# Two low weight halves moved in among the last residuals of a SwiGLU layer, and an earlier square root table load

## What is computed

```
def swiglu(h, w_in, w_out):
    g, u = jnp.split(h @ w_in, 2, axis=-1)
    return (jax.nn.silu(g) * u) @ w_out
...
x = x + 0.5 * swiglu(rms_norm(x, g), w_in, w_out)      # hidden width 2816
```

## Time and profile before

| what | value |
|---|---|
| median of 3 runs | 2894.66 us (2893.04 to 2894.82) |
| the profiled execution, whole | 2899.12 us |
| its span, first to last instruction | 2897.4 us |
| TensorE matmuls busy | 2780.8 us, 96% of the span |
| VectorE busy | 2065.6 us, 71% |
| ScalarE busy | 1025.2 us, 35% |
| TensorE's mean granted clock | 0.977 of full speed |
| HBM read | 418.94 MB, 145 GB/s over the span |

### The profile page before, as it was taken

The page is one execution under the profiler, slowest core; times in us unless marked ns, Lnnn a source line. Parts: engine busy times, 40 slices in busy tenths (PEclk is TensorE's granted clock), DMA queues, the critical chain, the costliest instruction groups (busy, mean ns, idle before and its releaser), DMA issues.

```text
span 2897.4 us, 49248 instructions
## 1 busy us (share of the span) xinstructions
PE 2780.8 (96%) x19380; PEld 2454.6 (85%) x19380; DVE 2065.6 (71%) x3075; ACT 1025.2 (35%) x1158; POOL 81.4 (3%) x152
## 2 busy tenths in 40 slices
PE   6999999999999999999999899998999999998999
PEld 4888877888878888788799899987799989986999
DVE  6877778867777777776667766656767766665677
ACT  5222224222232222233344444452144434443433
POOL 1000000000000000000000000000000000000000
PEclk9999999999999999999999999999999999998999
DMA  8444441443334444322245344421044544543354
GB/s 327 160 145 168 168 170 59 166 152 130 130 116 160 146 180 171 111 95 74 84 175 187 131 174 174 180 88 60 3 166 175 201 124 174 191 157 66 116 187 175
DMA packets 68705, 421.43 MB, mean 145 GB/s; under 512 B 7672, under 2 KB 8824, under 8 KB 26592
## 3 DMA queue, kind: packets, MB, share of 16 engines
q1 hardware_dynamic: 48032, 341.26, 31.8%
q0 software_dynamic: 20576, 78.78, 8.4%
HBM read 418.94 MB, written 1.07 MB: 145 GB/s over the span
## 4 chain that ended last, share of the span: by engine, by line
PE 86%; DVE 7%; issue 2%; ACT 2%; DMA 1%; DVEq 0%; SPq 0%; ACTq 0%
PE ps_o L2158 11%; PE ps_o L2159 10%; PE ps_o L2160 10%; PE ps_g L2158 7%; PE ps_u L2158 7%; PE ps_u L2159 7%; PE ps_u L2160 7%; PE ps_g L2159 7%; PE ps_g L2160 7%; PE ps_g L2173 2%; DVE wlo L1203 2%; ACT whi L708 1%; DMA wraw<-in_W 1%; PE ps_o L2378 1%; PE ps_o L2364 1%
## 5 line engine op out<-in xcount | busy, mean ns | idle before, releaser
L708 ACT ACTIVATE whi<-wraw 128x2048 fp32r<-128x2048 f32 x323 | 616.2, 1911 | 785.9 <-PE ps_u L2160 367.5
L1203 DVE TENSOR_TENSOR wlo<-wraw,whi 128x2048 fp32r<-128x2048 f32 x323 | 731.5, 2287 | 159.8 <-ACT whi L708 159.5
L2158 PE MATMUL ps_o<-ah,wlo 128*128 128x256 f32 (+1 forms) x1408 | 466.6, 331 | 12.2 <-issue 7.6
L2158 PE MATMUL ps_g<-hh,wlo 128*128 128x256 f32 (+1 forms) x1464 | 464.3, 317 | 12.5 <-ACT tsq L823 7.4
L2158 PE MATMUL ps_u<-hh,wlo 128*128 128x256 f32 (+1 forms) x1464 | 462.1, 316 | 0.3 <-DVE wlo L1203 0.2
L2160 PE MATMUL ps_g<-hh,whi 128*128 128x256 f32 (+1 forms) x1464 | 461.9, 315 | 0.0
L2159 PE MATMUL ps_g<-hl,whi 128*128 128x256 f32 (+1 forms) x1464 | 461.9, 315 | 0.0
L2159 PE MATMUL ps_u<-hl,whi 128*128 128x256 f32 (+1 forms) x1464 | 461.7, 315 | 0.0
L2160 PE MATMUL ps_u<-hh,whi 128*128 128x256 f32 (+1 forms) x1464 | 461.7, 315 | 0.0
L2159 PE MATMUL ps_o<-al,whi 128*128 128x256 f32 (+1 forms) x1408 | 455.6, 324 | 0.0
L2160 PE MATMUL ps_o<-ah,whi 128*128 128x256 f32 (+1 forms) x1408 | 455.4, 323 | 0.0
(11 more groups left out here) (456 smaller groups left out, 3726.6 us busy)
## 6 DMA issues: line engine op xcount, KB each, us to landing
wraw<-in_W SPq DMA_DIRECT2D x324, 1024.0 KB, 4.8
scr<-in_ADA POOLq DMA_DIRECT2D x126, 512.0 KB, 3.7
scr<-bias_rows POOLq DMA_DIRECT2D x8, 384.0 KB, 8.5
x<-in_XT POOLq DMA_DIRECT2D x1, 2048.0 KB, 10.4
x<-in_MEMT POOLq DMA_DIRECT2D x2, 1024.0 KB, 6.3
cst<-in_CST POOLq DMA_DIRECT2D x1, 1511.5 KB, 7.2
cst<-in_CB POOLq DMA_DIRECT2D x1, 1024.0 KB, 5.1
scr<-in_PM POOLq DMA_DIRECT2D x1, 1024.0 KB, 5.1
```

The source lines that it names most:

```text
L708: nc.scalar.activation(whi[:, n % SLOTS, :], wraw[:, n % SLOTS, :], ACT.Copy).then_inc(w_hi, 1)
L1203: tt_(wlo[:, n % SLOTS, :], wraw[:, n % SLOTS, :], whi[:, n % SLOTS, :].bitcast(f32), sub).then_inc(w_lo, 1)
L2158: mm(out, a[1], b[0], start=first, stop=False)
```

## The change

In layers 3 to 7 alone. On ScalarE a one-column square root stands behind the last SiLU of the layer. On VectorE the low half of the next stage's first chunk stands behind residual 3 of `n_down` and not behind residual 7, and the low half of the second stands behind residual 2 of `n_last` and not ahead of its residual 0.

```
                     silu(i * step + DONE[n0 + 2], i + (g0 + 1), i + (lg + 2))
                     if f in LATE:
                         split_hi(n0 + 5, i, step, per)
+                    nc.scalar.activation(cols[:, 61:62], C("eps", 1), ACT.Sqrt)
                     hidden(i + (g0 + 1), last_hi)
                     split_hi(n0 + 6, i, step, per)
                     split_hi(n0 + 7, i, step, per)
...
                     down(n_down, done, range(1))
                     hidden(i + (g0 + 1), last_hi, last_lo)
-                    down(n_down, done, range(1, KT))
+                    down(n_down, done, range(1, 4))
                     split_lo(n_up + SLOTS, i, per)
+                    down(n_down, done, range(4, KT))
+                    down(n_last, DONE[n_last - 1], range(3))
                     split_lo(n_down + SLOTS, i, per)
-                down(n_last, DONE[n_last - 1])
+                    down(n_last, DONE[n_last - 1], range(3, KT))
+                else:
+                    down(n_last, DONE[n_last - 1])
                 st["late"].append(n_last + SLOTS)
```

## The result

| | before | changed | ratio, 95% interval |
|---|---|---|---|
| first comparison, median | 2894.74 us (4 runs) | 2874.31 us (4 runs) | 0.9925 (0.9908 to 0.9942) |
| second comparison, median | 2895.9 us (11 runs) | 2875.35 us (6 runs) | 0.9929 (0.9914 to 0.9944) |
| span of the profiled execution | 2897.4 us | 2873.9 us | |

The change wins 20.4 us in the medians; 22.6 were forecast. To see where, I measure each layer's end alone: from the start of the last product on VectorE (line 1337 before, 1338 after) to the start of the last residual. In layers 3 to 7 that was 19.65, 18.96, 19.25, 18.86 and 15.34 before, and is 15.35, 13.61, 15.27, 13.60 and 12.38 now.

The account below looks back on a forecast made before the run. TensorE bounds 86% of the span, so time is won where it waits or runs at half clock. Layers 3 to 7 give 4.4 + 5.5 + 4.05 + 5.4 + 3.2 = 22.55 off the median 2894.66: 2872.1 us, range 2868 to 2881.

Parts of the forecast that it names:

- What set the wait: Layer ends: VectorE's low halves set TensorE's wait in layers 4 and 6 (2.90 in 4), ScalarE in 3 and 5 (3.54).
- Low B's place: Second chunk's low half behind residual 2 of n_last: runs 1843.04 to 1845.24 in layer 4, no wait at sum 3.
- The new wait at tile 0: First output tile of n_last, layer 4: starts at 1840.38 instead of 1839.89, a wait of 0.49, bounds 0 to 0.6.
- the hand-over from VectorE to TensorE: n_last's first tile in layer 4: TensorE starts it 0.06 behind the end of VectorE's residual 4.
- it would not fall behind 1.6 us: Layers 3 and 5: 1.6 us of idle time stays, TensorE keeps full clock; gains 4.4 and 4.05.
- rival 2: Timed runs lose clock less often than the profiled one: gain 18, 2876.6 us; chance 0.12.
- rival 1: Layers 3 and 5 still fall to half clock with 1.6 us idle: gain 16.9, 2877.8 us; chance 0.15.
- 3: Only the waits shrink, the clock falls all the same: gain 9.3, 2885.3 us; chance 0.06.
- 4: The time moves into the next stage, whose norm or low halves are late anyway: about 2894 us; chance 0.04.
- 5: Slower: first chunk's high half late, its low half holds up residuals 4 to 7; 7 us late gives 2907; chance 0.03.
- Rival 6: More gain: later idle stretches of 2 us or so keep their clock; three of them give 2867 us; chance 0.05.
- The early table load: ScalarE behind the last SiLU: load and one-column call, 1.48, fit into 3.00 idle in layer 5, cost nothing.

Follow-up runs that it names:

- early square root alone: Kernel before plus only the one-column square root behind the last SiLU on ScalarE: 2891.90 us, ratio 0.9986 to before.
- the order alone: Changed kernel without the one-column square root on ScalarE, so only VectorE's low halves moved: 2885.10 us, ratio 0.9962 to before.
- low B alone: Changed kernel with the first chunk's low half back behind residual 7 of n_down, the second's still moved: 2882.60 us, ratio 0.9946 to before.
- low A alone: Changed kernel with the second chunk's low half back ahead of residual 0 of n_last, the first's still moved: 2883.91 us, ratio 0.9957 to before.
- The added matmuls: Kernel before, with TensorE multiplying constants into an unused bank during the wait in layers 3 to 7: 2890.09 us, ratio 0.9978 to before.
- low A two earlier still: Changed kernel with the first chunk's low half two residuals earlier, ahead of residuals 2 and 3 of n_down too: 2884.17 us, ratio 0.9957 to before.
- the second profile of before: Kernel before, unchanged, profiled once more: 2894.62 us (one run), ends of layers 3 to 7 sum to 88.27 against 92.06 in its first profile.

## Why the prediction was right, point by point

*What set the wait.* Shown. In layers 4, 6 and 7 it was VectorE's low halves ahead of residual 0; in 3 and 5 ScalarE's memory squares and table load. In 3 and 5 neither part takes the wait away alone: 3.02 is left in layer 3 with the early square root, and 2.83 with the order. Each part of the change moved just the waits that it was said to.

*Which half matters.* Low B's place is the main part at the layer ends (71.3 with it alone, 75.8 with low A alone, 92.1 or 88.3 with neither), and the early square root is worth 0.7 in layers 4 and 6 and 1.4 of wait in 3 and 5. In layer 3 it also kept the clock up; in layer 5 that profile had no fall to save.

*The new wait at tile 0.* In layer 4 tile 0 was forecast to start 0.49 later. Counted from the last product it starts 0.57 later (5.97 behind it, before 5.40): VectorE's residual 4 is on time, but TensorE starts 0.14 behind the end of it and not 0.06. The trace shows 0.36 of this as idle time. Then the first matmul takes 0.19 to the next start where 0.12 is usual, another 0.08. So the first sum stands at 1836.28, where the forecast is 1836.12 on this scale. Layer 7 has two such waits (0.41 and 0.25), which fits its 2.96 where 3.2 was forecast. That is the mis-sized term: the hand-over from VectorE to TensorE was taken as 0.06, by the 0.03 seen at ScalarE, and the slow restart was put at nothing.

*The clock.* That the waits made it fall, and that it would not fall behind 1.6 us (1.38 and 1.41 in the trace) was right in both profiles of the changed kernel. The added matmuls show the cause by itself: with TensorE busy the clock stayed up in all five ends. How surely a wait costs the clock is less fixed than I took it. In layer 7, 2.45 made it fall in the first profile, 2.45 and 2.43 left it alone in two others. 2.90 and 3.54 cost it in every profile that had them, but not for the same time; 2.84 in layer 5 of the order alone did not, and 1.78 did in layer 3 with low A two earlier still. The first profile of before already held a warning that the prediction leaves out: 2.53 kept its clock at 412, and behind the same 2.53 at 828 the granted clock was 0.52. So the step from 1.81 to 1.6 ("I take full clock") was a likely choice and not a rule: that it held in layers 3 and 5 of both profiles is in part luck.

*The size.* The forecast of 2872.1 was 2.2 below the measured median. Of that, 0.7 is the ends, which gave 21.85 and not 22.55. The rest fits rival 2 in part: I took the sum from a profile in which all five ends lost their clock, and the second profile of before shows 3.8 less. How often the timed runs lose it is not shown, since they have no traces.

*No rival 1, 3, 4 or 5.* The clock stayed, the next stages took nothing back (1.7 more came than the ends gave, and TensorE's idle time in the norm behind layer 4 is 0.68 in both kernels), and high A was in time: low A has no idle time ahead of it in any of the five layers. *Rival 6* is not seen either: outside the ends TensorE was at half clock for about as long as before, 96 and 100 us in the changed kernel's two profiles, 100 and 97 in those of before.

*The early table load.* Covered, by 1.49 in the tightest layer. The load took 1.28 and the next call came 0.02 behind it. The Trainium skill, "ScalarE: Activation LUTs", section "What ACT_TABLE_LOAD costs", charges 2.66 a switch; the trace doesn't agree, since by that only 0.1 would have been left idle and not 1.49.

*Open.* Against the changed kernel, low B alone is 6.5 us slower in its median than its layer ends say, and early square root alone 2.8 faster than its waits say. Between executions of one kernel the time outside the ends moves by 4 us and more (2803.6 and 2808.0 for the changed kernel), with the granted clock. From layer 3's end to layer 4's last product the changed kernel took 192.7 at a granted clock of 1.00 in one profile and 194.3 at 0.99 in the other. It is the same in whole runs: of seventeen runs of before in one comparison the shortest, 2887.86, had a mean clock of 0.982, the longest, 2903.26, one of 0.977. I have not shown what decides at which idle stretches the clock falls, nor whether shifting the layer ends moves these falls in a steady way.

## What to carry to other kernels

Where an in-order engine both frees the matmul engine's output banks and prepares the next stage, put the preparation where the matmul engine is a full bank ring ahead, and as early as its own input allows but not earlier: here behind residual 3 and behind residual 2, two pieces of 2.2 us. Here a wait of TensorE of 2.5 to 3.5 us cost up to twice itself, since the work behind it could run at 1.2 GHz (layer 4: 2.90 of waiting and 2.8 of clock). Dummy matmuls in the wait tell the two apart; take more than one profile of the kernel that they are compared with. When a wait is gone, look next at the engine that ends last at the same place (here ScalarE with its memory squares), and move what doesn't have to be there.

## What was not expected of the hardware

The fall of TensorE's clock behind the same wait of the same program is not the same each time: layer 7's 2.45 us cost 1.4 us in one execution and nothing in another, layer 4's 2.90 cost 2.8 and 1.6 (against the 16.13 with TensorE kept busy). Nor does the longer wait always cost more: the clock fell once behind 1.78 us and stayed up once behind 2.84. Profiles of one execution each can therefore differ by 4 us at five places without any edit. And the matmul that restarts behind a wait of 0.36 or 0.41 us (layers 4 and 7 of the changed kernel) is followed 0.19 later by the next, where 0.12 is usual.
